# Running sums and score products of a float32 transformer kernel, written as single-pass products of a high and a low part

## What is computed

```
# retention, per head h, summed up over all earlier tokens
o_t = sum_{s<=t} gamma_h^(t-s) (q_t . k_s) v_s
# then o is normalised over its 512 columns, times silu(g), times w_out

# stick-breaking, per head, strictly causal
A[t,s] = sigmoid(z_ts) * prod_{s<j<t} (1 - sigmoid(z_tj)),  s < t
o_t = sum_s A[t,s] v_s       # then times silu(g), times w_out
```

## Time and profile before

| what | value |
|---|---|
| time, median of 3 runs | 1845.34 us (1839.01 to 1845.58) |
| the profiled execution's own time | 1843.15 us |
| its span, first to last instruction | 1841.3 us |
| mean granted TensorE clock | 0.988 |
| PE busy | 1773.2 us |
| DVE busy | 1008.2 us |
| ACT busy | 665.4 us |
| data moved by DMA | 147.70 MB, mean 80 GB/s |

### The profile page before, as it was taken

The page is one execution under the profiler, slowest core; times in us unless marked ns, Lnnn a source line. Parts: engine busy times, 40 slices in busy tenths (PEclk is TensorE's granted clock), DMA queues, the critical chain, the costliest instruction groups (busy, mean ns, idle before and its releaser), DMA issues.

```text
span 1841.3 us, 23445 instructions
## 1 busy us (share of the span) xinstructions
PE 1773.2 (96%) x9653; PEld 1448.0 (79%) x9653; DVE 1008.2 (55%) x1490; ACT 665.4 (36%) x996; POOL 177.2 (10%) x152
## 2 busy tenths in 40 slices
PE   6799998999999999999999999999999999999997
PEld 5577776779779888888898777878798777777786
DVE  3667789455435972964875544435456433344435
ACT  4344343355345332321362222222245434243352
POOL 0053544210010000000010000000010000000001
PEclk9899999899999999999999999999999999999999
DMA  5111112233121322332332222322222222222221
GB/s 185 39 47 47 36 59 69 68 113 106 58 71 57 102 91 94 111 106 79 106 109 92 65 102 69 101 83 81 69 84 70 68 80 69 80 81 69 79 71 46
DMA packets 44937, 147.70 MB, mean 80 GB/s; under 512 B 4768, under 2 KB 8736, under 8 KB 44832
## 3 DMA queue, kind: packets, MB, share of 16 engines
q1 hardware_dynamic: 44832, 146.21, 24.3%
HBM read 144.09 MB, written 2.10 MB: 79 GB/s over the span
## 4 chain that ended last, share of the span: by engine, by line
PE 87%; DVE 9%; ACT 2%; issue 1%; DMA 0%; POOL 0%; SPq 0%; DVEq 0%; ACTq 0%; POOLq 0%
PE ps L422 29%; PE ps L417 19%; PE ps L418 19%; PE ps L419 19%; DVE acc L1984 2%; DVE sl L1793 1%; DVE ca L1844 1%; DVE y L2162 0%; PE ps L1008 0%; DMA raw<-in_wqkv 0%; DVE pad L1835 0%; ACT sh L1163 0%; DVE ss L1950 0%; DVE ca L1840 0%; DVE acc L2410 0%
## 5 line engine op out<-in xcount | busy, mean ns | idle before, releaser
L1163 ACT ACTIVATE sh<-raw 128x1024 fp32r<-128x1024 f32 x260 | 271.4, 1054 | 537.4 <-PE ps L419 413.8
L1793 DVE TENSOR_TENSOR sl<-raw,sh 128x1024 fp32r<-128x1024 f32 x260 | 323.2, 1253 | 150.3 <-ACT sh L1163 150.1
L417 PE MATMUL ps<-xh,sh 128*128 128x512 f32 x640 | 264.1, 413 | 0.0
L419 PE MATMUL ps<-xl,sh 128*128 128x512 f32 x640 | 252.9, 395 | 0.0
L418 PE MATMUL ps<-xh,sl 128*128 128x512 f32 x640 | 252.7, 395 | 0.0
L417 PE MATMUL ps<-sh,xh 128*128 128x512 f32 x384 | 161.0, 419 | 0.1
L419 PE MATMUL ps<-sl,xh 128*128 128x512 f32 x384 | 150.1, 391 | 0.0
L418 PE MATMUL ps<-sh,xl 128*128 128x512 f32 x384 | 149.8, 390 | 0.0
L417 PEld LDWEIGHTS ps<-xh,sh 128*128 128x128 f32 x640 | 122.6, 191 | 27.3 <-issue 2.1
L419 PEld LDWEIGHTS ps<-xl,sh 128*128 128x128 f32 x640 | 122.2, 191 | 26.6
L418 PEld LDWEIGHTS ps<-xh,sl 128*128 128x128 f32 x640 | 122.7, 192 | 24.9 <-issue 1.7
(11 more groups left out here) (353 smaller groups left out, 3236.1 us busy)
## 6 DMA issues: line engine op xcount, KB each, us to landing
raw<-in_wup SPq DMA_DIRECT2D x44, 512.0 KB, 3.5
raw<-in_wdn SPq DMA_DIRECT2D x24, 512.0 KB, 3.4
raw<-in_rqk SPq DMA_DIRECT2D x16, 512.0 KB, 4.0
raw<-in_rv SPq DMA_DIRECT2D x16, 512.0 KB, 3.5
raw<-in_rg SPq DMA_DIRECT2D x16, 512.0 KB, 4.4
raw<-in_rout SPq DMA_DIRECT2D x16, 512.0 KB, 3.5
raw<-in_sv SPq DMA_DIRECT2D x16, 512.0 KB, 3.4
raw<-in_sg SPq DMA_DIRECT2D x16, 512.0 KB, 3.5
```

Of the source, the lines that this page charges most:

```text
L417: e.matmul(dst, wh, ah, start=start, stop=False, skip_group_check=True)
L419: return e.matmul(dst, wh, al, start=False, stop=stop, skip_group_check=True)
L1163: e.activation(SH[j % NSPL][:], RAW[j % NRAW][:], ACT.Copy).then_inc(*hi(j))
L1793: e.tensor_tensor(SL[j % NSPL][:], RAW[j % NRAW][:], SH[j % NSPL][:].bitcast(F32), ALU.subtract).then_inc(*lo(j))
```

## The change

Retention: ACT writes the high part of the scores to `SPLIT` and of the values to `VH`, DVE the differences to `SCL` (in the place of `SC`) and `VL`. The outputs are formed by `three` from these. ACT now stores the high part of all four blocks of values, and DVE the low part of all four. The value blocks of head 0 take the PSUM banks 6, 5, 4, 7 instead of 6, 5, 0, 1. `SQB` takes the place of `TM` in part. DVE's gate products may be done block by block, and PE's transposes wait for them block by block.

Stick-breaking: ACT writes the high part of the first three blocks of `SP` (1152 columns) to `SPLIT`, DVE the difference to `SPL` in place. The running sums of these blocks are two fp32r products each, with the ones in fp32r (`ONR`, `LWR`; a one has no low part). The last block of 128 columns stays one float32 product, for each s. ACT and DVE do their extra step within the four ticks that lay between scores and sums; DVE's addition to `SP` moves one tick later.

Groups: in `group` and `boundary` the third slab runs one k behind the first two (not in the first group of the program and in the one on `WOUT_K`), so that there is one round more.

```diff
-        VR, GR = QK0, ACC
+        GR = ACC
+        SPLIT = under("split", [128, 1280], F32R)
+        VH = under("vh", [128, 4, T], F32R)
+            SCL = under("scl", [128, 1280], F32R)
+            VL = alloc(ph, "vl", [128, NB, T], F32R)
-            SQB = [alloc(ph, f"sqb{i}", [128, T]) for i in range(4)]
+            SQB = TM + [alloc(ph, "sqb", [128, T])]
-        RVB = ((6, 5, 0, 1), (0, 1, 2, 3), (0, 1, 2, 3), (0, 1, 2, 3))
+        RVB = ((6, 5, 4, 7), (0, 1, 2, 3), (0, 1, 2, 3), (0, 1, 2, 3))
...
-            def group(j0, moving, banks, nk=8, mt=1, ks=None, pre=None, post=None):
+            def group(j0, moving, banks, nk=8, mt=1, ks=None, pre=None, post=None, lag=(0, 0, 1)):
+                for r in range(nk + max(lag[:len(moving)])):
+                    now = [(i, r - lag[i], *m) for i, m in enumerate(moving) if 0 <= r - lag[i] < nk]
...
-                    for k in range(8):
+                    for r in range(9):
+                        now = [(i, r - i // 2, *m) for i, m in enumerate(moving) if 0 <= r - i // 2 < 8]
...
-                    pe.wait_ge(*rtv[("sc", h, 3)])
+                    pe.wait_ge(*rtv[("sl", h, 3)])
                     for s in range(tb + 1):
-                        t = one(b[:], SC[:, o:o + 128], VR[:, s, :], s == 0, s == tb)
+                        t = three(b[:], SPLIT[:, c], SCL[:, c], VH[:, s, :], VL[:, s, :], s == 0, s == tb)
...
-                    pe.wait_ge(*rtv[("g", h, 3)])
                     for tb in range(NB):
+                        pe.wait_ge(*rtv[("g", h, tb)])
...
-                    pe.wait_ge(*stv[("sp", p, h)])
-                    for q in range(s, NB):
-                        m = (4 - q) * 128
-                        t = one(b[:, n - m:n], LOW[:] if q == s else ONE[:], SP[:, SOFF[q]:SOFF[q] + m], q == s, q == 3)
+                    for i, part in enumerate((SPLIT, SPL)):
+                        pe.wait_ge(*(stv[("sl", p, h)] if i else sta[("sh", p, h)]))
+                        for q in range(s, 3):
+                            m = (4 - q) * 128
+                            one(b[:, n - m:n], LWR[:] if q == s else ONR[:], part[:, SOFF[q]:SOFF[q] + m],
+                                i == 0 and q == s, False)
+                    t = one(b[:, n - 128:n], LWR[:].bitcast(F32) if s == 3 else ONE[:], SP[:, SOFF[3]:], s == 3, True)
...
+                    ac.wait_ge(*rtv[("sc", h, s)])
+                    e.activation(SPLIT[:, c], SC[:, c], ACT.Copy).then_inc(*rta(("sh", h, s)))
...
-                for tb in (0, 2):
+                for tb in range(NB):
-                    e.activation(VR[:, tb, :], PS[RVB[h][tb]][:], ACT.Copy, scale=RC[:, tb:tb + 1]).then_inc(*rta(("v", h, tb)))
+                    e.activation(VH[:, tb, :], PS[RVB[h][tb]][:], ACT.Copy, scale=RC[:, tb:tb + 1]).then_inc(*rta(("v", h, tb)))
...
+                ac.wait_ge(*stv[("sp", p, h)])
+                e.activation(SPLIT[:, LONG], SP[:, LONG], ACT.Copy).then_inc(*sta(("sh", p, h)))
...
+            def score_lo(h, s):
+                ve.wait_ge(*rta[("sh", h, s)])
+                e.tensor_tensor(SCL[:, c], SC[:, c], SPLIT[:, c].bitcast(F32), ALU.subtract).then_inc(
+                    *rtv(("sl", h, s)))
...
-                for tb in (1, 3):
-                    e.tensor_scalar(VR[:, tb, :], PS[RVB[h][tb]][:], RC[:, tb:tb + 1], None, ALU.mult).then_inc(
+                for tb in range(NB):
+                    e.scalar_tensor_tensor(VL[:, tb, :], PS[RVB[h][tb]][:], RC[:, tb:tb + 1],
+                                           VH[:, tb, :].bitcast(F32), ALU.mult, ALU.subtract).then_inc(
...
+                ve.wait_ge(*sta[("sh", p, h)])
+                e.tensor_tensor(SPL[:, LONG], SP[:, LONG], SPLIT[:, LONG].bitcast(F32),
+                                ALU.subtract).then_inc(*stv(("sl", p, h)))
```

More of the change, by code:

```diff
@@ L170, in alloc, with under @@
             return stack.enter_context(nc.sbuf_tensor(name, shape, dt))
+        def under(name, shape, dt):
+            with ExitStack() as ph:
+                return alloc(ph, name, shape, dt)
         PS = [root.enter_context(nc.psum_tensor(f"ps{i}", [128, 512], F32)) for i in range(8)]
@@ L244, in program @@
             ZZS = [alloc(ph, f"zz{i}", [128, 1280]) for i in range(2)]
+            SPL = under("spl", [128, 1280], F32R)
             SP = alloc(ph, "sp", [128, 1280])
+            ONR = alloc(ph, "onr", [128, 128], F32R)
             BIG = alloc(ph, "big", [128, 128])
+            LWR = under("lwr", [128, 128], F32R)
             LOW = alloc(ph, "low", [128, 128])
@@ L445, in slab @@
                             beat()
-            def group(j0, moving, banks, nk=8, mt=1, ks=None, pre=None, post=None):
+            def group(j0, moving, banks, nk=8, mt=1, ks=None, pre=None, post=None, lag=(0, 0, 1)):
                 dst = [[PS[i] for i in b] for b in banks]
                 ks = ks or range(nk)
[L451 to L454, removed]
+                for r in range(nk + max(lag[:len(moving)])):
+                    if r < nk and pre:
+                        pre(ks[r])
+                    now = [(i, r - lag[i], *m) for i, m in enumerate(moving) if 0 <= r - lag[i] < nk]
+                    for i, q, X, src in now:
+                        k = ks[q]
                         wait_x(pe, src, k)
@@ L464, in group @@
                             one(dst[i][m][:], wl[:, k, c], X[0][:, k, :], False, False)
-                    for i, (X, src) in enumerate(moving):
+                    for i, q, X, src in now:
                         wh = views(j0 + i, 128 * mt)[0]
@@ L517, in x_sums @@
                 sums(("x", k), 7, 0, SQ[k % 2], sq[("x", k)], k == 0, k == 7)
-            group(0, [(X, "x")] * 3, [[0], [1], [2]], post=x_sums)
+            group(0, [(X, "x")] * 3, [[0], [1], [2]], post=x_sums, lag=(0, 0, 0))
             rel[7] = [(ms, "x")]
@@ L823, in tensor_program @@
             side.drain()
-            group(40, [(X2, "2mix")] * 3, [[1], [2], [0]], ks=WOUT_K)
+            group(40, [(X2, "2mix")] * 3, [[1], [2], [0]], ks=WOUT_K, lag=(0, 0, 0))
             rel[1], rel[2], rel[0] = [(ya, ("y1", 0))], [(ya, ("y1", 1))], [(ya, ("y1", 2))]
@@ L860, in boundary @@
                     c = TH[hf]
-                    for k in range(8):
-                        if not hf and k == (5 if b == 3 else 3):
+                    for r in range(9):
+                        if not hf and r == (5 if b == 3 else 3):
                             y_sums(b, 1)
-                        for i, (X_, src) in enumerate(moving):
+                        now = [(i, r - i // 2, *m) for i, m in enumerate(moving) if 0 <= r - i // 2 < 8]
+                        for i, k, X_, src in now:
                             wait_x(pe, src, k, hf)
@@ L1596, in retain @@
             def retain(h):
-                for _ in range(NB):
+                for s in range(NB):
+                    c = slice(SOFF[s], SOFF[s] + (4 - s) * 128)
+                    ac.wait_ge(*rtv[("sc", h, s)])
+                    e.activation(SPLIT[:, c], SC[:, c], ACT.Copy).then_inc(*rta(("sh", h, s)))
                     yield
@@ L1687, in weights @@
                     ac.wait_ge(*stm[("c", p if h else p - 1, 0 if h else 1, 3)])
[L1688 removed]
+                F = SP[:]
+                e.activation(F, ZZ[:], ACT.Abs).then_inc(*sta(("abs", p, h)))
                 ac.wait_ge(*sta[("abs", p, h)])
[L1690 removed]
+                e.activation(F, F, ACT.Exp, scale=-1.0).then_inc(*sta(("exp", p, h)))
                 ac.wait_ge(*sta[("exp", p, h)])
[L1692 to L1693 removed]
+                e.activation(F, F, ACT.Ln, bias=1.0).then_inc(*sta(("ln", p, h)))
+                for _ in range(2):
+                    yield
+                ac.wait_ge(*stv[("sp", p, h)])
+                e.activation(SPLIT[:, LONG], SP[:, LONG], ACT.Copy).then_inc(*sta(("sh", p, h)))
+                for _ in range(2):
                     yield
@@ L1732, in scalar_program @@
                 if p == 0:
+                    ac.wait_ge(*d_sb["low"])
+                    e.activation(ONR[:], ONE[:], ACT.Copy)
+                    e.activation(LWR[:], LOW[:], ACT.Copy).then_inc(*sta("lwr"))
                     rg_end = used[at[("rg", 15)]]
@@ L2387, in retain, with gate @@
                         ve.wait_ge(*rtm[("o", h - 1, 3)])
-                    e.tensor_tensor(SC[:, SOFF[s]:SOFF[s] + n], PS[4 + s % 2][:, 0:n], DD[:, 0:n], ALU.mult).then_inc(
-                        *rtv(("sc", h, s)))
-                    yield
+                    e.tensor_tensor(SC[:, SOFF[s]:SOFF[s] + n], PS[4 + s % 2][:, 0:n], DD[:, 0:n],
+                                    ALU.mult).then_inc(*rtv(("sc", h, s)))
+                    if s:
+                        score_lo(h, s - 1)
+                    if s == 3:
+                        score_lo(h, 3)
+                    yield
+                gates = list(range(NB))
+                def gate(n):
+                    while len(gates) > n:
+                        tb = gates.pop(0)
```

(14 more changed lines are left out.)

36 lines of the change are left out of this document (23 added, 13 removed).

## The result

The changed kernel takes 1823.63 us, median of 4 runs (1820.6 to 1825.56); the kernel before in the same comparison 1844.18 (1839.01 to 1845.58). The ratio is 0.9892 with a 95% interval from 0.9867 to 0.9917, that is 20.5 us less at the medians. The forecast was 1825.3 in a range from 1819 to 1832, and "faster". The profiled execution took 1824.85 us over a span of 1822.9; the one before 1843.15 over 1841.3.

A forecast was written before the change was run, and what follows sets the result against it. The prediction took PE to bound the kernel. Running sums -12.6, score products -6.8, odd-head gates +0.8 and boundary lag +0.7 summed to -17.9, from 1843.15 to 1825.3 us, range 1819 to 1832.

The forecast's parts named there:

- What bounds the kernel: Retention and the stick-breaking heads are PE-bound; ACT and DVE have room, so their extra work costs nothing.
- Running sums: Stick-breaking: ten float32 products per head become twelve single-pass and four float32, saving 1.58 us per head, 12.6 over eight.
- Score products: Retention: 40 float32 products each give way to three single-pass ones, saving 6.8 us.
- Gates and waits at the odd heads: Retention, before PE's transposes: waiting for DVE's gate products loses net 0.4 us, twice, 0.8 in all.
- Cover of the new steps: ACT's and DVE's splitting finishes before PE needs it; two stick-breaking heads might stall 0 to 0.5 us each, taken as 0.
- The lag in the boundaries: Boundaries: PE would wait for `XL` anyway, so the third slab's lag loses 0.36 us at each, 0.7 together.
- the lag helps: Rival, boundaries: both PE waits go and the 1.5 us are not paid, some 1822.5 us; chance 0.12.
- weight loads: Rival, slower: 216 single-pass products each take 0.19 us longer, 41 us in all, 1866 us; chance 0.02.
- four-pass products: Rival: split products stay four-pass; 80 further float32 products in retention add 69 us, about 1920 at least; chance 0.01.
- half gain: Rival: split products at upper prices, 1 us stall per thin head, 3 us for the lag: -10.7, 1832.5 us; chance 0.11.

The follow-up runs named there:

- lag_only: Only the lag of the third slab in `group` and `boundary` added to the kernel before, all products as before: 1842.1 us, ratio 0.9989.
- ret_only: Only retention's score-value products split, with block-wise gates and waits and no lag, against the kernel before: 1833.43 us, ratio 0.995.
- short_block: The changed kernel with the last block of 128 columns split too, in single-pass products: 1824.33 us in one run.

## Why the prediction was right, and where it was not

**What bounds the kernel**: right. PE was streaming on both sides of the change, so PE work counted in full and 44 us of new work on ACT and DVE did not count.

**Running sums**: 12.6 predicted, 12.38 measured. The 384-column product, whose price I had laid between two others at 0.175, is 0.18 by the two starts shown above.

**Score products**: 6.8 predicted, 6.4 measured (1.6 per head in the heads where nothing else changed). The chain had shown 0.23 to 0.24, and I took 0.23; 10 x (0.86 - 3 x 0.233) = 1.6 gives the measured value.

**Gates and waits at the odd heads**: +0.8 predicted, +0.8 measured (1.61 - 1.22 and 1.59 - 1.21, by the stretches). lag_only and ret_only show its two halves, +1.45 and -0.7.

One sign named for it did not come as said: no single wait ahead of the transposes grew to 1.3 us; PE idles 0.81 there, in the three pieces shown above.

**Cover of the new steps**: right, with little to spare in the two heads that the prediction had named. Last head of the changed kernel, DVE, then PE:

```profile
1747.26 1.36 DVE L2547 TENSOR_TENSOR spl<-sp,split 128x1152 fp32r<-128x1152 f32 x1 [0.72 <-ACT split L1726]
...
1748.47 0.40 PE L436 MATMUL ps<-split,lwr 128*128 128x512 f32 x1
...
1749.00 0.40 PE L436 MATMUL ps<-spl,lwr 128*128 128x512 f32 x1
```

The low part is ready at 1748.62, PE comes for it at 1749.00: 0.4 us. It is 0.4 in the second head of the first pair too, and 2.4 to 3.3 in the other six.

**The lag in the boundaries**: the step that failed, with the wrong sign. I put 0.7 us of loss; it is 2.1 of gain. The step read "PE's next round starts at 948.12, right after `XL` of block 1 is ready at 947.59 + 0.48". That instruction does not write block 1. DVE's program puts the second difference of block k into step k+2 and the third slab behind step 3, so block 1 comes ahead of the slab. The timeline of DVE before shows all of it:

```profile
942.73 0.48 DVE L2179 SCALAR_TENSOR_TENSOR xl<-h,prm,xh 128x256 fp32r<-128x256 f32 x1 [0.67 <-ACT xh L1207]
...
945.00 0.48 DVE L2179 SCALAR_TENSOR_TENSOR xl<-h,prm,xh 128x256 fp32r<-128x256 f32 x1
945.39 0.41 DVE L2154 TENSOR_TENSOR y<-y,ps 128x256 f32<-128x256 f32 x1
945.73 1.22 DVE L1793 TENSOR_TENSOR sl<-raw,sh 128x1024 fp32r<-128x1024 f32 x1
```

Those at 942.73 and 945.00 are blocks 0 and 1; the one at 947.59 is block 2, and PE had no need of it at 948.12. That PE's round starts just after it is a coincidence: the round follows the four short products of the row sums, which start at 947.76, without an idle stretch. So the slab was the only thing PE waited for, and the lag gives PE block 1 of the first two slabs to do meanwhile. The sign that the prediction named, that the waits would move from the slab to `XL`, did not come. After the change PE goes on with its own work until 947.93, and then has its next start 0.32 later instead of 0.12, so that some 0.2 of the idle 1.23 is left (DVE, then PE):

```profile
946.16 0.48 DVE L2216 SCALAR_TENSOR_TENSOR xl<-h,prm,xh 128x256 fp32r<-128x256 f32 x1
...
946.88 1.22 DVE L1830 TENSOR_TENSOR sl<-raw,sh 128x1024 fp32r<-128x1024 f32 x1
...
947.93 0.29 PE L436 MATMUL ps<-xh,sl 128*128 128x256 f32 x1
948.25 0.35 PE L436 MATMUL ps<-xh,sh 128*128 128x256 f32 x1
```

The rival "the lag helps" (0.12) was the better account of this part. That the time came out so close, 1824.85 for the profiled execution and 1825.3 forecast, is in part luck: the 2.8 us of this step are made up for by 1.7 that the first 420 us of this one profile took more, and by 0.6 of terms taken a little too high. Without the first 420 us the change is worth 20.2 us, and I had summed up 17.9.

**The other rivals.** Neither the weight loads nor four-pass products show: the distance of 0.23 us at 512 columns excludes both. Of the half gain nothing came but prices of up to 0.24 at 512 columns; there were no stalls, and the lag did not cost 3 us.

**The rule of the Trainium skill** that a weight load overlaps only with matmuls of another row group (TensorE: Matmul & The Clock Gate, Part 3, The mechanism), taken by itself, does not hold for this kernel: loads of 128 columns take 0.19 us in the records, and products of 256 columns still follow each other at 0.12.

What stays open: why the two first boundaries gain 0.3 us each from the lag, where no idle PE shows; and what makes the first 420 us vary, the clock or something behind it. Neither was followed up.

## What to carry to other kernels

Where PE streams without a gap, price products by the distance of starts in the chain, and a change of pass counts can be forecast to a few per cent: three single-pass products save a fifth of a float32 one at 512 columns, two (where one operand is exact) some 45% (0.47 for 0.86 at 512 columns, 0.24 for 0.44 at 256), and at 128 columns two save nothing. Before calling two neighbouring times cause and effect, count in the code which instance of a repeated instruction each one is. A lag or a shift that helps in one place should be tried place by place, since the same lag cost at the heads two thirds of what it earned in the boundaries.

## What the runs showed of the hardware

Between the ten kernels, the stretches whose code is the same agree within 0.1 us over 1400 us, with the clock at 1.00; all of the 6 us of spread in them came from the first 420 us, where the granted clock is 0.93 to 0.97 on average. A single-pass product of 128 columns cost 0.11 us on average (short_block), less than the 0.19 that its weight load shows in the records, and hardly less than one of 256 columns, 0.12.
